# Attention in fp32 halves: scores packed into fewer matmul passes, the running maximum in two PSUM banks, and a row of maxima copied by DMA

## What is computed

```python
def block(q_blk):
    s = (jnp.einsum('bqhd,bkhd->bhqk', q_blk[..., :QK_NOPE], k_nope)
         + jnp.einsum('bqhr,bkr->bhqk', q_blk[..., QK_NOPE:], kpe))
    p = jax.nn.softmax(s.astype(jnp.float32) * scale, axis=-1).astype(v.dtype)
    return jnp.einsum('bhqk,bkhd->bqhd', p, v)
```

## Time and profile before

| | us |
|---|---|
| median of 3 runs | 3606.66 |
| the profiled execution | 3599.82 |
| its span | 3598.1 |
| attention, from the first maximum products to the last exponential | 1082.3 to 2081 |
| busy in the whole span: PE, PEld, DVE, ACT, POOL | 3151.8, 2498.3, 2034.8, 1059.1, 1040.6 |

### The profile page before, as it was taken

The page is one execution under the profiler, slowest core; times in us unless marked ns, Lnnn a source line. Parts: engine busy times, 40 slices in busy tenths (PEclk is TensorE's granted clock), DMA queues, the critical chain, the costliest instruction groups (busy, mean ns, idle before and its releaser), DMA issues. The chain is left out here.

```text
span 3598.1 us, 44483 instructions
## 1 busy us (share of the span) xinstructions
PE 3151.8 (88%) x17218; PEld 2498.3 (69%) x17218; DVE 2034.8 (57%) x2246; ACT 1059.1 (29%) x1410; POOL 1040.6 (29%) x619
## 2 busy tenths in 40 slices
PE   8999999993878999999999949979962999999991
PEld 7888888881446666666666627768851899999991
DVE  3427557384447677767767625444456455555553
ACT  3411111112333333333333322123320333333332
POOL 0000000001002333333333342223311855555551
PEclk7999999996888999999999979989975999999995
DMA  4313122222240101110010034554411566666656
GB/s 174 113 37 130 49 100 80 81 99 77 63 101 19 23 5 23 23 23 5 23 23 5 6 133 149 167 209 160 163 57 63 176 192 192 192 192 192 192 151 229
DMA packets 131647, 368.44 MB, mean 102 GB/s; under 512 B 17616, under 2 KB 41952, under 8 KB 120832
## 3 DMA queue, kind: packets, MB, share of 16 engines
q1 hardware_dynamic: 89248, 259.69, 22.1%
q0 software_dynamic: 22080, 73.51, 7.2%
q10 hardware_dynamic: 20160, 33.04, 2.4%
HBM read 263.17 MB, written 102.91 MB: 102 GB/s over the span
## 5 line engine op out<-in xcount | busy, mean ns | idle before, releaser
L1067 DVE TENSOR_REDUCE at_mpart<-at_mx 128x4 f32<-128x1024 f32 (+1 forms) x291 | 351.2, 1207 | 241.5 <-PE at_mx L1001 240.5
L932 ACT ACTIVATE at_w<-at_sc 128x1024 f32<-128x1024 f32 (+1 forms) x296 | 299.5, 1013 | 564.9 <-PE at_sc L981 533.3
L960 POOL TENSOR_TENSOR at_part<-at_part,at_w 128x512 f32<-128x512 f32 x224 | 297.9, 1330 | 450.9 <-ACT at_w L932 449.8
L1880 POOL TENSOR_TENSOR moe_gu_lo<-moe_raw_gu,moe_gu_hi 128x2048 fp32r<-128x2048 f32 x64 | 297.9, 4660 | 134.8 <-ACT moe_gu_hi L1919 134.4
L492 DVE SCALAR_TENSOR_TENSOR fr_r<-fr_r,fr_dw 128x2334 f32<-128x2334 f32 x120 | 318.0, 2650 | 3.9
L367 PE MATMUL fr_po<-hT_hi,fr_w_hi 128*128 128x512 f32 (+1 forms) x800 | 297.4, 372 | 2.1 <-PE fr_tp L367 1.2
L367 PE MATMUL fr_po<-hT_lo,fr_w_hi 128*128 128x512 f32 (+1 forms) x800 | 295.0, 369 | 0.0
L367 PE MATMUL fr_po<-hT_hi,fr_w_lo 128*128 128x512 f32 (+1 forms) x800 | 294.9, 369 | 0.0
L1013 PE MATMUL at_acc<-at_w,V 128*64 128x256 f32 (+1 forms) x2368 | 288.9, 383 | 0.0
L1092 DVE TENSOR_TENSOR at_part<-at_part,at_w 128x512 f32<-128x512 f32 x224 | 239.9, 1071 | 25.0 <-ACT at_w L932 13.7
L1997 DVE TENSOR_TENSOR moe_d_lo<-moe_raw_d,moe_d_hi 128x1024 fp32r<-128x1024 f32 x64 | 190.2, 2972 | 107.5 <-ACT moe_d_hi L1940 105.5
(11 more groups left out here) (316 smaller groups left out, 6987.2 us busy)
## 6 DMA issues: line engine op xcount, KB each, us to landing
moe_raw_gu<-w_gate_up SPq DMA_DIRECT2D x64, 1024.0 KB
moe_raw_d<-w_down SPq DMA_DIRECT2D x64, 512.0 KB
fr_wm<-w_ada_rows POOLq DMA_DIRECT2D x32, 512.0 KB, 4.6
gates_scratch<-fr_r ACTq DMA_DIRECT2D x64, 256.0 KB, 2.0
mx_gates<-gates_scratch SPq DMA_DIRECT2D x64, 256.0 KB, 3.9
fr_raw<-w_in SPq DMA_DIRECT2D x28, 512.0 KB, 4.4
fr_r<-x POOLq DMA_DIRECT2D x18, 512.0 KB, 4.5
op_m_raw<-mixed_scratch SPq DMA_DIRECT2D x9, 1024.0 KB, 5.6
```

Of the source, the lines that this page charges most:

```text
L932: act.activation(w[:, g % NW, :, 0:n], sc[:, 2 * (g % 2):2 * (g % 2) + 2, 0:n], ACT.Exp, scale=SM_SCALE).then_inc(exp_done, 1)
L960: pool.tensor_tensor(part[:, j % 2, 1, 0:n], before, w[:, g % NW, 1, 0:n], ALU.add).then_inc(add_p, 1)
L1067: dve.tensor_reduce(mpart[:, 0:q, c], max_bank(m)[:, 0:q, :], AX.X, ALU.max).then_inc(red_done, 1)
L1880: pool.tensor_tensor(gu_lo[:, slot], raw_gu[:, slot], gu_hi[:, slot].bitcast(F32), ALU.subtract).then_inc(glo_done, 1)
```

## The change

The stacking of rows is new. With 64 + 32 elements split in two, three products of 96 rows are 288 rows. The new kernel lays 256 of them out as two matmuls of all 128 rows (`ka` by `qa`, `kb` by `qb`) and the rest, 32 rotary rows of high key by low query and the row of maxima, as a matmul of 33 rows (`kr` by `qr`). The rests of a step's two key tiles stand on partitions 0 to 32 and 64 to 96, that is in the upper and lower half of the array, and go to two banks. `rests` runs for both steps of a pair ahead of their scores.

The stacks need copies on other partitions. SyncE makes four by DMA per head (`copy_keys`, `copy_queries`: 64 x 2560, 32 x 2304, 64 x 2304 and 32 x 2304 elements), and ScalarE issues a DMA (`copy_row`) that copies each row of maxima from partition 32 to 96. The low parts of the keys move from VectorE to GpSimd (`split_keys`, two operations of 32 x 640 a piece), those of the queries stay on VectorE as two operations a piece (`split_queries`, 64 x 576 and 32 x 576).

`mx` is now used as two separate banks: products and reductions go bank by bank, each with its own semaphores. LA goes from 11 to 13. The turn writes to bank 1 alone; where it stood ahead of both `values` it now stands between them.

```diff
-    LA = 11
+    LA = 13
-        mx = p.ps("mx", [P, 4, 256])
+        mx = p.ps("mx", [P, 2, BLK])
+                def copy_keys(h):
+                    u = h % 2
+                    sp.wait_ge(hi_piece, PIECES * h + (4 if h else PIECES))
+                    sp.dma_start(kb[u][NOPE:P, :].bitcast(F32), ka[u][0:NOPE, :].bitcast(F32)).then_inc(copied, 16)
...
+                def copy_row(j):
+                    tok, n = BLOCKS[j % BH]
+                    act.wait_ge(row_done, j + 1)
+                    row = qr[j // BH % 2]
+                    act.dma_start(row[NOPE + ROPE:NOPE + ROPE + 1, tok:tok + n].bitcast(F32),
+                                  row[ROPE:ROPE + 1, tok:tok + n].bitcast(F32)).then_inc(row_copied[j % 2], 16)
...
+                    m = g - 2 + LA
+                    if g >= 2 and m <= G and (m == G or STEPS[m][2] == 0):
+                        copy_row(block_of(m - 1))
...
+                def split_keys(h, r):
+                    u, c = h % 2, cut(r)
+                    pool.wait_ge(hi_piece, PIECES * h + (r if h else FIRST.index(r)) + 1)
+                    for i, dst in enumerate((ka[u][HQ:P, c], kb[u][0:ROPE, c])):
+                        at, n = i * ROPE, 8 * h + 2 * r + i
+                        wait(pool, klo_piece, n)
+                        pool.tensor_tensor(dst, raw_k[at:at + ROPE, c], ka[u][at:at + ROPE, c].bitcast(F32), ALU.subtract
+                                           ).then_inc(klo_piece, 1)
...
+                def rests(g):
...
                     if g == 1:
-                        pe.wait_ge(red_done, LA)
+                        for half in range(2):
+                            pe.wait_ge(red_done[half], LA)
                     if c == 0:
                         pe.wait_ge(row_done, block_of(g) + 1)
+                        pe.wait_ge(row_copied[block_of(g) % 2], 16 * (block_of(g) // 2) + 16)
...
+                    for k in range(2):
+                        rows = slice(k * NOPE, k * NOPE + ROPE + 1)
+                        pe.matmul(sc[:, 2 * (g % 2) + k, 0:n], kr[rows, half:half + P], qr[u][rows, tok:tok + n],
+                                  start=True, stop=False)
...
-                        pe.matmul(bank, k_hi[u][:, keys], q_hi[u][:, tok:tok + n], start=True, stop=False)
-                        pe.matmul(bank, k_lo[u][:, keys], q_hi[u][0:HQ, tok:tok + n], start=False, stop=False)
-                        mm = pe.matmul(bank, k_hi[u][0:HQ, keys], q_lo[u][:, tok:tok + n], start=False, stop=True)
+                        pe.matmul(bank, ka[u][:, keys], qa[u][:, tok:tok + n], start=False, stop=False)
+                        mm = pe.matmul(bank, kb[u][:, keys], qb[u][:, tok:tok + n], start=False, stop=True)
...
+                    for half in range(2 if b < NB else 1):
+                        if half == 0:
+                            wait(pe, red_done[0], m - 1 if m < LA else m)
+                        else:
+                            wait(pe, red_done[1], FULL[m - 1] if 0 < m < LA else FULL[m])
+                            wait(pe, row_done, block_of(m))
+                        for i in range(2):
+                            at = tok + (2 * half + i) * P
+                            mm = pe.matmul(max_bank(m, half)[:, i, :], qa[u][0:HQ, at:at + P], ka[u][0:HQ, k0:k0 + 256],
+                                           start=True, stop=True)
+                        mm.then_inc(m_mm[half], 1)
...
                     for i in (g, g + 1):
+                        rests(i)
+                    for i in (g, g + 1):
                         scores(i)
...
+                    halves = 2 if b < NB else 1
+                    for half in range(halves):
+                        dve.wait_ge(m_mm[half], m + 1 if half == 0 else FULL[m + 1])
+                        dve.tensor_reduce(mpart[:, 2 * half:2 * half + 2, c], max_bank(m, half), AX.X, ALU.max
+                                          ).then_inc(red_done[half], 1)
```

More of the change, by code:

```diff
@@ L1040, in _ @@
                     late = g + 1 + LA
-                    if late <= G and (late == G or STEPS[late][2] == 0):
-                        turn_max(block_of(late - 1))
-                        turned = True
-                    else:
-                        turned = False
-                    if late < G and not turned:
-                        max_products(late)
-                    for i in (g - 2, g - 1):
-                        if i >= 0:
-                            values(i)
-                    if late < G and turned:
+                    turn = late <= G and (late == G or STEPS[late][2] == 0)
+                    if late < G and not turn:
+                        max_products(late)
+                    if g:
+                        values(g - 2)
+                    if turn:
+                        turn_max(block_of(late - 1))
+                    if g:
+                        values(g - 1)
+                    if late < G and turn:
                         max_products(late)
```

148 lines of the change are left out of this document (87 added, 61 removed).

## The result

The changed kernel takes 3622.11 us, the median of 20 runs (3612.73 to 3630.24), against 3610.79 (3599.55 to 3622.30) of the kernel before on the same chips: a ratio of 1.0031 [1.0021, 1.0042], 11.3 us slower. The forecast was 8 us faster; the range held the time, the direction was wrong. The profiled executions are 3617.05 after and 3599.82 before, with spans of 3615.4 and 3598.1.

The account below looks back on a forecast made before the run. TensorE was taken to set the pace, VectorE close behind. Pairs -33, query splits +8, even block ends +7, copied row +7 and start +3 summed to -8 us, from 3606.66 to 3598.7; range 3550 to 3655.

Parts of the forecast that it names:

- Start: First reduction to first score: VectorE's chain of 13 reductions and 8 short splits plus the turn gets longer, +3 us.
- Bounds, packing, change of tiling, two banks: Regular pair of steps: TensorE sets the pace, rests overlap in twos, 6.07 us becomes 5.88; together -33 us.
- Query splits: 28 pairs with a query piece: VectorE has 6.0 to 7.0 us of work in 5.88, 0.3 each, +8 us.
- Even turns: Ends of even blocks: the turn ahead of the pair's matmuls waits 0.35 longer for VectorE, 20 times, +7 us.
- Odd turns: Ends of odd blocks: the turn between the values saves a wait of about 0.3 but costs two tiling changes; even.
- Copied row: Row of maxima copied by DMA: rests of blocks beginning at odd steps wait 0.35 for it, 20 times, +7 us.
- The row's own rival: Copied row lands late, after 4 us instead of 2, delaying blocks at odd and even steps; 3659 us, chance 0.06.
- serial rests: Rival: the rests' matmuls run one after the other, +70 us over the pairs, net +62; 3669 us, chance 0.12.
- VectorE becomes the bound: Rival: GpSimd's splits beside additions lengthen them; VectorE exceeds the pair in 28 query pairs, +37; 3628 us, chance 0.20.
- long additions: Sign of being wrong, in the new profile: additions (L1175) with a mean above 1.4 us.
- The free change of tiling: Rival: in each pair the third tiling change costs nothing and the waits are absent; 3565 us, chance 0.16.

Follow-up runs that it names:

- e1: Changed kernel with GpSimd's two rotary subtractions of 32 x 2560 at the start cut into eight of 32 x 640; 3613.40 us, ratio 1.0015.
- e2: Changed kernel with the first rotary subtraction in four pieces ahead of GpSimd's key pieces, the second in four pieces in the step loop; 3610.74 us, ratio 1.0008.
- e13: Changed kernel with look-ahead back from 13 to 11 steps, the row's copy issued behind the same exponential; 3663.79 us.
- e12: e9 with VectorE's query subtractions one to a pair instead of two, and at the start behind GpSimd's pieces; 3571.41 us, ratio 0.9891.
- e5: Changed kernel with both rests of a step taken from partitions 0 to 32, the same rows of the array (output changes); 3689.88 us.
- e4: Changed kernel with the maximum as before the change: four products into both banks, one reduction of 128 x 1024, one semaphore; 3667.24 us.
- e3: Changed kernel with the turn of the maximum in odd pairs put back ahead of both value bursts; 3616.98 us, ratio 1.0028.
- e9: e2 with VectorE's two additions behind both reductions in every pair where no block's sums are taken; 3581.49 us, ratio 0.9917.
- e6: Changed kernel with GpSimd's additions on 8 of the 512 columns, half of the row sums left out; 3561.99 us.
- e7: Kernel before the change with GpSimd's additions on 8 of the 512 columns, half of the row sums left out; 3569.99 us.
- e11: Kernel before the change with VectorE's additions behind both reductions unless sums are due; 3598.62 us, ratio 0.9952.

## Why the prediction was wrong

**The step that failed is the term "Start": +3.** It counted the reductions and eight short splits and set beside them that "GpSimd's prologue, 8 x 1.66 + 6.6 for the rotary keys = 20 us from about 1076, ends before". Measured +16.1. The sum has a slip, since the kernel has two rotary operations of 6.0 us each and not one: the prologue took 26.1 us, from 1081.50 to 1107.63. But the step would have failed without it. GpSimd's work was treated as running in parallel, to be late or not, and what costs is that VectorE's operations on two SBUF operands do not run beside it, while the reductions that TensorE waits for stand behind them. The experiments e1 (-5.7) and e2 (-8.2) show this by moving GpSimd's operations alone; e13 puts 2.4 on the look-ahead. That leaves 16.1 - 8.2 - 2.4 = 5.5. In e2 three splits still took 1.97 where 0.75 is their free length, 3.7 in all; in e12, where the surplus of two is 1.7, the start is 1.9 shorter, which agrees. Some 2 us are left. Half of them lie behind the block's last reduction (L1152): from there to the first exponential it is 10.19 us after and 6.76 before, of which e13 puts 2.4 on the look-ahead. The other half lies ahead of it, on VectorE; neither is separated further.

With 3 in place of 16.1, and all else as measured, the kernel would have been 2 us faster than before, a draw: this term alone made a loss of it. The other 6 us between the forecast and that draw are a balance: odd turns +11.2, queries and even turns +6.4 over their terms, against -7 for the row, -3 for the pair and -1 for the rest.

A second thing was put at nothing without a reason: TensorE's clock in the loop. The prediction read the full clock in one regular stretch and priced each wait at its own length. Behind waits that the change made longer the clock fell, so that 33.1 us of the loop are at the lower level instead of 13.7, worth 7 to 10 us by the estimates above, nearly the size of the whole loss. It is contained in the turns and in plain pairs behind them.

The other steps, in their order:
- *Bounds, packing, change of tiling, two banks*: forecast 5.88 a pair, measured 5.80. Rests to products 1.72 against 1.70, first to second products 1.40 against 1.41, the wait on the second bank 0.24 against 0.18. Held; e5 shows the overlap of the rests (0.46 forecast as 0.47), e4 the worth of the banks (0.42). The sum of it, -33, became -36.
- *Query splits* (+8): +11.5. Right mechanism, a little larger; e12 makes it smaller by spreading the splits.
- *Even turns* (+7): +9.9. Right mechanism. The wait for VectorE's last reduction grew from the earlier trace rows's 24.9 to 31.6, in fewer and longer waits (19 with the longest 2.2, before 26 with the longest 1.8), and the longer ones are those behind which the clock fell.
- *Odd turns* (0): +11.2. The gain of an earlier turn came to nothing. e3 shows that its place on TensorE does not matter, e9 that VectorE's order does. Why VectorE is late there is read, not tested: the two exponentials of a pair now start 1.41 apart (1462.09 and 1463.50) and not 1.86 (1458.44 and 1460.30), so GpSimd's two additions can run back to back (1729.24 above), and both of VectorE's meet them.
- *Copied row* (+7): 1.2 us of waits. The landing took 1.7 and the rests of odd blocks found it there. The row's own rival (0.06) is out too.
- *Rivals*: serial rests are out by e5. "VectorE becomes the bound" named GpSimd and VectorE in each other's way and gave 3628 against 3622 measured, which is luck, for it had the wrong place: it put +37 on the 28 query pairs, where +11.5 arose, and spoke of the loop only. The long additions it named as its sign (mean above 1.4 us) did not come (1.20); GpSimd's additions took the gain all the same, 23 us by e6 and e7 with the clock's part, and what counts is not the mean addition but the one ahead of a turn. The free change of tiling is not borne out by the pair of 5.80.

The rule that bears on the failed step is in the Trainium skill, "SBUF — State Buffer", section "Who interferes with whom": a VectorE instruction with two SBUF inputs contends with a GpSimd instruction that reads SBUF, and the shared port pair is an exclusive lock. The trace agrees: 6.01 and 4.82 us for an operation of 0.75, each ending just behind one of GpSimd's, and 0.64 per reduction from PSUM throughout. By that rule the start could have been laid out beforehand as a chain: each two-operand operation of VectorE ends no earlier than the GpSimd operation that was running when it came.

What stays open: the last 2 us at the start, that the waits bring the clock down (read from their order in the traces and from e6, e7 and e11, not tested by itself), what besides a long wait decides whether the clock falls behind it, how much of each loop's difference the clock makes beyond the two estimates, and how e13's 51 us divide between DMA and turn.

## What to carry to other kernels

Where VectorE and GpSimd both read two operands from SBUF, count their times as a sum and not side by side, and look at what stands behind VectorE's operation in its queue; one of 6 us held a subtraction of 0.75 for nearly its whole length, and cut into pieces the same work cost 5.7 us less. When work is taken off the engine that sets the pace, the gain is paid out only where the next engine in the chain is on time: here 36 us in the regular pairs and nearly nothing in total, until reductions went ahead of additions and the splits were spread, which made it some 40, of which the new order alone gives the old kernel 13. A wait of TensorE of 1.1 to 2.5 us, as here, can cost more than its length, because its clock may fall to half behind it: read the granted clock of every loop that is compared, also where its mean looks full (0.99 and 0.98 here). A one-row copy by DMA with slack is free where the same row written by the busy engine costs 25 us.

## What the runs showed of the hardware

- VectorE's subtraction of 32 x 576 took 0.75 us free, 1.97 beside GpSimd operations of 32 x 640 and 6.01 beside one of 32 x 2560. Its reductions from PSUM did not change.
- Four matmuls of 33 rows in two row halves, two by two in different banks, take 0.67 us until the next full matmul, and 1.12 on the same rows: rests on different rows stream at the same time. Less two passes of 0.233, some 0.2 of the 0.67 is left for the change of shape and the first weight load, an estimate.
- GpSimd's additions taken away left the regular pair as it was (5.80 and 5.79 us) and yet shortened the loop by 58 us, 42 of it in pairs with a turn or a piece of queries.
- A DMA of one row of 512 elements from partition 32 to 96 landed 1.7 us after its issue.
- TensorE's granted clock fell from 1.00 to 0.50 inside a loop in which it was busy 94% of the time, behind waits of 1.1 to 2.2 us (after) and of 2.5 us (e9, where ten us at 0.50 followed). The loops had 0 to 114.8 us at the lower level, and two profiles of the same instructions 33.1 and 54.1.
